# Batched 64-token triangular inverses of an RWKV layer: all four quadrants of the PE array, two tiles half a level apart

## The reference, cut to what matters

```python
def step(state, inp):
    r_t, w_t, k_t, v_t, kk_t, a_t = inp
    sa = jnp.einsum('bhvk,bhk->bhv', state, kk_t)
    state = (state * w_t[:, :, None, :]
             - sa[..., None] * (kk_t * a_t)[:, :, None, :]
             + v_t[..., None] * k_t[:, :, None, :])
    return state, jnp.einsum('bhvk,bhk->bhv', state, r_t)
...
_, y = lax.scan(step, state0, xs)
```

## Time and profile before

| what | us |
|---|---|
| median of 3 runs (2185.68 to 2186.8) | 2185.74 |
| the profiled execution: its time | 2186.04 |
| the profiled execution: span of its instructions | 2184.3 |
| PE busy in the span | 2126.0 |
| first product of round 0, from the span's start | 534.21 |
| first product of round 1 | 569.27 |
| first product of the scan | 605.28 |

### The profile page before, as it was taken

How to read it: one execution, slowest core, us unless ns; L and a number is a source line. 1 busy time by engine, 2 the same in 40 slices (tenths; PEclk the granted TensorE clock), 3 DMA queues, 4 the chain that set the end, 5 groups by cost and what they waited for, 6 DMA issues and landing times. The chain is left out here.

```text
span 2184.3 us, 33539 instructions
## 1 busy us (share of the span) xinstructions
PE 2126.0 (97%) x13592; PEld 1752.4 (80%) x13592; DVE 1134.0 (52%) x1435; ACT 767.3 (35%) x1059; POOL 175.8 (8%) x122
## 2 busy tenths in 40 slices
PE   7999999989989999999999999999999999999998
PEld 6888888768967888888888888877888778888886
DVE  5444444568756544444444444377766665444322
ACT  4222223463333322222322222254554443233221
POOL 2000011001502000001000001101111110000010
PEclk9999999999999999999999999999999999999999
DMA  4222322310012222333222232221111122222321
GB/s 166 96 96 96 122 93 68 108 58 21 5 60 78 96 96 96 103 107 98 77 96 96 96 118 93 78 88 49 40 40 50 50 68 97 96 96 96 116 93 52
DMA packets 48271, 182.75 MB, mean 84 GB/s; under 512 B 6320, under 2 KB 6576, under 8 KB 48048
## 3 DMA queue, kind: packets, MB, share of 16 engines
q1 hardware_dynamic: 48176, 181.39, 25.1%
HBM read 179.27 MB, written 2.10 MB: 83 GB/s over the span
## 5 line engine op out<-in xcount | busy, mean ns | idle before, releaser
L570 PE MATMUL banks<-H,WS 128*128 128x512 f32 x1840 | 733.6, 399 | 13.4 <-DVE H L1763 9.7
L571 PE MATMUL banks<-H,WS 128*128 128x512 f32 x1840 | 719.9, 391 | 0.0
L572 PE MATMUL banks<-H,WS 128*128 128x512 f32 x1840 | 719.8, 391 | 0.0
L1167 ACT ACTIVATE WS<-RAW 128x1024 fp32r<-128x1024 f32 (+1 forms) x310 | 349.1, 1126 | 961.0 <-PE banks L572 956.0
L1683 DVE TENSOR_TENSOR WS<-RAW,WS 128x1024 fp32r<-128x1024 f32 (+1 forms) x310 | 405.3, 1308 | 228.1 <-ACT WS L1167 227.8
L570 PEld LDWEIGHTS banks<-H,WS 128*128 128x128 f32 x1840 | 347.6, 189 | 94.0 <-DVE WS L1683 12.0
L572 PEld LDWEIGHTS banks<-H,WS 128*128 128x128 f32 x1840 | 347.4, 189 | 73.7
L571 PEld LDWEIGHTS banks<-H,WS 128*128 128x128 f32 x1840 | 347.5, 189 | 71.1 <-issue 2.4
L570 PE MATMUL banks<-A,WS 128*128 128x512 f32 x704 | 273.9, 389 | 0.0
L571 PE MATMUL banks<-A,WS 128*128 128x512 f32 x704 | 273.9, 389 | 0.0
L572 PE MATMUL banks<-A,WS 128*128 128x512 f32 x704 | 273.9, 389 | 0.0
(11 more groups left out here) (360 smaller groups left out, 1734.1 us busy)
## 6 DMA issues: line engine op xcount, KB each, us to landing
RAW<-in_w_gate SPq DMA_DIRECT2D x88, 512.0 KB, 3.4
RAW<-in_w_up SPq DMA_DIRECT2D x88, 512.0 KB, 3.4
RAW<-in_w_down SPq DMA_DIRECT2D x64, 704.0 KB, 4.0
RAW<-in_c_in SPq DMA_DIRECT2D x32, 512.0 KB, 3.4
RAW<-in_ab_in SPq DMA_DIRECT2D x22, 512.0 KB, 3.4
RAW<-in_ab_out SPq DMA_DIRECT2D x8, 512.0 KB, 4.0
RAW<-in_c_out SPq DMA_DIRECT2D x8, 512.0 KB, 3.5
X<-in_x SPq DMA_DIRECT2D x4, 512.0 KB, 7.3
```

The source lines that it names most:

```text
L570: pe.matmul(bank[:, :], WS[:, 0, s, cols], upper, start=first and j == 0, stop=False)
L571: pe.matmul(bank[:, :], WS[:, 0, s, cols], lower, start=False, stop=False)
L572: mm = pe.matmul(bank[:, :], WS[:, 1, s, cols], upper, start=False, stop=last and j == len(rows) - 1)
L1167: act.activation(WS[:, 0, c % SPLIT, 0:cols], RAW[:, c % RING, 0:cols], ACT.Copy).then_inc(hi_ready, 1)
```

## The change

- Chunks 4 to 7 of the inverse's matrices are stored on the opposite partition half. A product then sends half of its small products through the off-diagonal quadrants (`four_ways`). Outputs lie in half banks: chunks 0 to 3 in the first and 4 to 7 in the second bank of a pair (`head_block`, `two_banks`).
- XX is turned by three DVE transposes in place of one (`turned_across`).
- The pair masks go from TM (POOL, each level) to U (DVE, on the way out of PSUM: `minus_by_head`). POOL makes TM once for each tile and round (`triangle`); DVE makes XT from it (`first_turn`).
- PE's order: U of tile 0, XX of tile 1 of the level before, one extra product (`beside`), U of tile 1, XX of tile 0, one extra product. The products of `matrices` and `inside` are spread over the levels; round 1's first product stands in level 4 of round 0.
- The turns of KF go ahead of the levels of round 0, those of AL ahead of and into round 1 (not crossed).
- `branch`, `branch_lo` and `fold` go from DVE to POOL. BV goes ahead of the last `z_block`, one factor product (AL) from block 20 to block 19. The first products don't wait for the last `z_block`. The third `bon_mm` product waits for two copies of the turned VF.
- In the scan the operands of chunks 4 to 7 are read from the other half.

Left out below: the small helpers of the half banks, the semaphore table, most removed lines (they stand in the functions above), and the wrappers of three copies.

```diff
@@ -635,46 +643,52 @@
...
+            lo_half, hi_half = slice(0, CHUNK), slice(CHUNK, P)
+            four_ways = [(r, crossed(r) if c >= TT else r, c) for k in range(TT) for c in (k, TT + k) for r in (lo_half, hi_half)]
...
+            def tokens_turned(first, src, b, upper, across):
...
+                for r, a, c in four_ways:
+                    tr = pe.matmul(head_block(first, a if across else r, c, upper), src[r, b, c * CHUNK:(c + 1) * CHUNK],
+                                   con("ident")[r, r], start=True, stop=True)
                 tr.then_inc(tr_mm, 1)
...
+            def pe_level_u(q, z, l):
+
+                w = INV[z]
+                if l == 0:
+                    pe.wait_ge(x1_turned[z], q + 1)
+                    pe.wait_ge(tm_ready[z], q + 1)
+                    if q == 0:
+                        pe.wait_ge(tr_read, (8, 6)[z])
+                    elif z == 0:
+                        pe.wait_ge(xx_read[z], 5)
                     else:
-                        pe.wait_ge(xx_read[z], 5 * q + l)
...
+                        pe.wait_ge(tr_read, 10)
+                    for r, c in chunk_blocks():
+                        mm = pe.matmul(head_block(4 * z, r, c), w["TM"][r, c, :], w["XX"][r, c, :], start=True, stop=True)
+                else:
+                    pe.wait_ge(xx_read[z], 5 * q + l)
+                    for a, f, c in four_ways:
+                        mm = pe.matmul(head_block(4 * z, f, c), w["TM"][a, c, :], w["XX"][a, c, :], start=True, stop=True)
+                mm.then_inc(u_mm[z], 1)
+
+            def pe_level_xx(q, z, l):
+
+                w = INV[z]
+                pe.wait_ge(iu_ready[z], 5 * q + l + 1)
+                if l:
+                    pe.wait_ge(xt_turned[z], 4 * q + l)
+                if l == 4:
+                    for r, c in chunk_blocks():
+                        mm = pe.matmul(head_block(4 * z, r, c, upper=True), w["IU"][r, c, :], w["XT"][r, c, :], start=True, stop=True)
+                elif l:
+                    for a, f, c in four_ways:
+                        mm = pe.matmul(head_block(4 * z, a, c, upper=True), w["XT"][f, c, :], w["IU"][f, c, :], start=True, stop=True)
+                else:
+                    for r, c in chunk_blocks():
+                        mm = pe.matmul(head_block(4 * z, r, c, upper=True), w["XT"][r, c, :], w["IU"][r, c, :], start=True, stop=True)
+                mm.then_inc(xx_mm[z], 1)
 
@@ -748,55 +762,96 @@
...
+                            for first, b in ((6, 0), (2, 2)):
                                 aux_free(20 + b)
-                                tokens_turned(aux_bank(20 + b), VF, b)
+                                aux_free(21 + b)
+                                tokens_turned(first, VF, b, upper=False, across=True)
+                                tokens_turned(first, VF, b + 1, upper=True, across=True)
...
+                                if b == 2:
+                                    pe.wait_ge(tr_read, 2)
...
-                    pe.wait_ge(z_read, AB_BLOCKS)
...
+                    def matrix(q, z, k):
...
+                        left, right = ((AL, CPRE), (KF, CPRE), (KF, RF), (AL, RF))[k]
+                        if k == 2:
+                            pe.wait_ge(token_read[z], 2 * q + 1)
+                        elif k == 3:
+                            pe.wait_ge(token_read[z], 2 * q + 2)
+                        elif q or k:
+                            pe.wait_ge(mat_ready[z], 4 * q + k)
                         elif z:
...
+                        for r, a, c in four_ways:
+                            cc = slice(c * CHUNK, (c + 1) * CHUNK)
+                            if k < 3:
+                                mm = pe.matmul(head_block(4 * z + 2, a, c), left[r, b, cc], right[r, b, cc], start=True, stop=True)
+                            else:
+                                mm = pe.matmul(BANK[4 * z + 2][r, cc], left[r, b, cc], right[r, b, cc], start=True, stop=True)
+                        mm.then_inc(mat_mm[z], 1)
...
+                    def inside(q, z, k):
...
+                        pe.wait_ge(mat_ready[z], 4 * q + 2 + k)
+                        for r, a, c in four_ways:
                             cc = slice(c * CHUNK, (c + 1) * CHUNK)
-                            mm = pe.matmul(BANK[4 * z + 1][r, cc], TKM[z][r, c, :], VT[r, b, cc], start=True, stop=True)
+                            if k == 0:
+                                mm = pe.matmul(head_block(4 * z + 2, r, c), TKM[z][a, c, :], VT[a, b, cc], start=True, stop=True)
+                            else:
+                                mm = pe.matmul(head_block(4 * z + 2, r, c), VT[a, b, cc], MKM[z][a, c, :], start=True, stop=True)
                         mm.then_inc(token_mm[z], 1)
...
+                    def beside(q, l, z):
+
+                        if l == 0:
+                            inside(q, z, 0)
+                        if l == 1:
+                            matrix(q, z, 2)
+                        if l == 2:
+                            inside(q, z, 1)
+                        if l == 3:
+                            matrix(q, z, 3)
+                        if l == 4 and q == 0:
+                            matrix(1, z, 0)
+                        if l == 4 and q:
+                            pe.wait_ge(mat_ready[z], 8)
+                            tokens_turned(4 * z + 2, AL, 2 + z, upper=False, across=False)
...
                     for q in range(2):
...
+                        if q == 0:
+                            matrix(0, 0, 0)
+                            matrix(0, 1, 0)
+                            tokens_turned(4, KF, 2, upper=False, across=True)
+                            tokens_turned(4, KF, 3, upper=True, across=True)
+                        matrix(q, 0, 1)
+                        matrix(q, 1, 1)
+                        if q == 0:
+                            pe.wait_ge(z_read, AB_BLOCKS)
+                            tokens_turned(0, KF, 0, upper=False, across=True)
+                            tokens_turned(0, KF, 1, upper=True, across=True)
+                        else:
+                            pe.wait_ge(xx_read[1], 5)
+                            tokens_turned(4, AL, 0, upper=False, across=False)
+                            tokens_turned(4, AL, 1, upper=True, across=False)
                         for l in range(5):
-                            pe_inverse_level(q, l, 4 * (q + 1), 2 * (q + 1))
+                            pe_level_u(q, 0, l)
+                            if l:
+                                pe_level_xx(q, 1, l - 1)
+                            beside(q, l, 0)
+                            pe_level_u(q, 1, l)
+                            pe_level_xx(q, 0, l)
+                            beside(q, l, 1)
+                        pe_level_xx(q, 1, 4)
@@ -818,6 +873,7 @@
@@ -827,7 +883,8 @@
...
+                                a = crossed(r) if c >= TT else r
+                                mm = pe.matmul(BANK[1][r, b * CHUNK:(b + 1) * CHUNK], KT[a, b, cc], VT[a, b, cc], start=True, stop=True)
@@ -1209,19 +1266,46 @@
...
+            def level_copied(q, z, l):
+
+                act.wait_ge(xx_mm[z], 5 * q + l + 1)
+                act.activation(by_head(INV[z]["XX"]) if l < 4 else row_by_head(XTF[:, 2 * q + z, :]), two_banks(4 * z, upper=True),
+                               ACT.Copy).then_inc(xx_read[z], 1)
...
             def act_inverse(q):
...
+                if q == 0:
+                    for b, written in ((2, 6), (3, 6), (0, 8), (1, 8)):
+                        tokens_copied(KT, b, 2 * b if b % 2 == 0 else 2 * b - 2, b % 2 == 1, written)
+                else:
+                    for b in range(2):
+                        tokens_copied(BT, b, 4, b == 1, 10)
                 for l in range(5):
...
+                    if l:
+                        level_copied(q, 1, l - 1)
+                    if l in (0, 2):
+                        inside_copied(q, 0, l // 2)
+                    if l == 4 and q:
+                        tokens_copied(BT, 2, 2, False, 11)
+                    level_copied(q, 0, l)
+                    if l in (0, 2):
+                        inside_copied(q, 1, l // 2)
+                    if l == 4 and q:
+                        tokens_copied(BT, 3, 6, False, 12)
+                    if q == 0 and l in (1, 3):
                         branch_hi(l - 1)
...
+                        branch_hi(l)
+                level_copied(q, 1, 4)
@@ -1611,26 +1688,31 @@
...
+            def triangle(q, z):
+
+                w = INV[z]
+                pool.wait_ge(mat_ready[z], 4 * q + 1)
+                if q:
+                    pool.wait_ge(u_mm[z], 5 * q)
+                pool.tensor_tensor(w["TM"][:, :, :], w["TT"][:, :, :], half("ident"), ALU.subtract).then_inc(tm_ready[z], 1)
...
+            def branch(b):
+
+                pool.wait_ge(silu_done, b + 1)
```

(99 more changed lines are left out.)

142 lines of the change are left out of this document (15 added, 127 removed).

## The result

| | before | after |
|---|---|---|
| median, us | 2185.71 (2184.36 to 2189.06, 6 runs) | 2178.41 (2175.68 to 2179.53, 6 runs) |
| profiled execution, us | 2186.04 | 2178.15 |
| ratio after/before | | 0.9967, interval 0.9957 to 0.9977 |

The change makes the kernel 7.3 us faster, against a forecast of 14.1. The sign was right; the time lies 1.4 us above the range of 2168 to 2177.

A forecast was written before the change was run, and what follows sets the result against it. It took the inverse, alone between projections and scan, as the bound, with PE's pace setting a level. Savings of -7.0 by round 0's first crossed turn grew to -14.55 by round 1's, -14.1 at the scan: 2171.6 us median, range 2168 to 2177.

The forecast's parts named there:

- The start: VF's turns to round 0's first product: crossed turns -1.65, a copy wait +0.5, no `z_block` wait; 532.2 instead of 534.21.
- the front of round 0: First product to level 1's first turn: 8 products ahead of U, not 12; turn at 543.0, -7.0 with the start.
- Prices: Unit costs: crossed product 0.52 us for 0.93, crossed turn with IU 1.38, XT 1.30 while POOL works, fold 2.2.
- Levels 1 to 4: Inverse levels: DVE cycle 3.96, PE and ACT cycle 4.16, masked level 5.16; 4.0 to 5.2 us against 4.99.
- PE's own work is at most 3.5: Levels 1 to 4: PE's work per level at most 3.5 us, below the cycles of 3.96 and 4.16.
- DVE idle in the levels: Sign that the forecast is wrong: DVE idling in the levels would mean that hops or PE decide.
- So these levels cost what they cost before: Round 1's levels and the end: from -14.55 at its first crossed turn to -14.1 at the scan, at 591.2.
- rival 1: Inverse levels: hand-overs slower than the rows, 0.2 instead of 0.1, two loops catching on each other; 2175 us, chance 0.14.
- Rival 2: Making XT on DVE isn't held up by POOL, 0.69 four times, -2.4 us; 2169 us, chance 0.09.
- Rival 3: Crossing doesn't pay because the quadrants don't run at once; level cycle 5.74 us, time 2184, no change; chance 0.05.
- Rival 4: PE's clock falls to 1.2 GHz within the inverse; level cycle 6.24 us, time 2193, slower; chance 0.04.
- The 25 ns of the Trainium skill: Matmul starts never closer than about 25 ns: crossed product 0.8 us, cycle 5.28, time about 2178; chance 0.02.

The follow-up runs named there:

- e2: Changed kernel with MKM, MBT and the second `inside` product issuing one of 16 small products each, 360 matmuls less, results not computed: 2172.32 us, ratio 0.9936.
- e11: The changed kernel run once more, unchanged: 2177.51 us, ratio 0.9966 (8 runs).
- e1: Changed kernel with each crossed product's small products reordered, so only two quadrants work at a time within one product: 2179.70 us, ratio 0.9971.
- e6: Changed kernel plus 32 crossed products of 64 columns (1024 matmuls), waiting for nothing, just ahead of the scan: 2212.89 us.
- e8: Changed kernel plus 32 uncrossed products of 64 columns (two quadrants), waiting for nothing, just ahead of the scan: 2212.68 us.
- e4: Changed kernel with only the first of the crossed turn's three DVE transposes left, XT of chunks 4 to 7 staying old: 2179.01 us, ratio 0.9965.
- e7: Changed kernel plus 32 crossed products of 128 columns, waiting for nothing, just ahead of the scan: 2207.85 us.
- e5: Changed kernel with TKM and MKM merged into wider matmuls and unread chunk 7 turns left out, 160 matmuls less, all results kept: 2174.25 us, ratio 0.9951.
- e9: Changed kernel with the burst of 32 crossed products of 64 columns ahead of the scan, executed a second time unchanged: 2208.07 us.
- e10: Changed kernel with the burst of 32 crossed products of 128 columns ahead of the scan, executed a second time unchanged: 2210.61 us.
- e3: Changed kernel with MKM, MBT and the second `inside` product issued twice, 384 matmuls more, results kept: 2191.25 us, ratio 1.0025.

## Why the forecast was half right

- **The start** (2.3 shorter, forecast 2.0) and **the front of round 0** (11.06, forecast 10.8): right, by the steps given. The third `bon_mm` product waited 0.86 for ACT's copies.
- **Prices**: crossed product 0.47 to 0.52, crossed turn 0.44 + 0.89 with IU 1.38 behind its start, XT under POOL 1.29, 1.66 and 1.86 (one of four 0.68, begun 0.17 us before POOL's next piece), a fold 1.68 to 2.13 (estimate 2.2): right, and the last fold ended before the scan. That XT was sometimes over 1.30 cost nothing that can be seen: e2 has it too.
- **Levels 1 to 4: the step that failed.** "PE's own work is at most 3.5" priced PE by the array's time. A level issues six products, 192 matmuls, 1.5 blocks; at 3.65 that is 5.5 us, above both loops of the forecast (3.96 on DVE, 4.16 through ACT) and above the masked level (5.16). From level 1 to level 4 that is 4.5 blocks, 16.4 us; the trace has 17.2 in round 0 (541.11 to 558.32) and 16.5 in round 1 (572.83 to 589.33), where the forecast had 14.6. Most of it came in level 3 (7.5 and 6.2 for 5.2), where DVE waits for the MBT products. (These are not crossed, so that even the array needs 4 x 0.52 + 2 x 0.93 = 3.9 in that level, not "at most 3.5".) The forecast's own sign, DVE idle in the levels, is there: 7.6 us of waits between 541 and 596. So PE's instruction stream sets the pace in both rounds' levels wherever extra products stand in them, and in round 1's front. The sum for the whole inverse is 18 x 3.65 = 65.6 where the forecast had 59.0: 6.6 us, nearly the whole miss (66.8 in e11, 18 x 3.71). The 3.65 isn't only this quotient: PE goes on after the first stop at 533.75 and after the last at 588.58, 15 blocks later, 3.66 each. e2 shows it from the other side: 2.8 blocks fewer, 58.8.
- **"So these levels cost what they cost before"** (the end, 20.7): 22.84. The forecast put extra products into round 1's levels as free filling. They were the costly part.
- **Where the 7.3 come from.** 2.3 from the start, of which 0.6 is lost again in e1 (18.33 in place of 17.69), and 5.5 from the inverse. How the 5.5 divide between the quadrants and the order isn't shown: e1 takes back only half of the crossing (and loses 1.3 by the medians), and no run has uncrossed products in the new order. In the bursts crossing gains 1.8 us of 31.1 (e6 against e8), and before the change the inverse took 4.0 us more than its uncrossed products need (71.1 for 18 x 3.73 = 67.1). That speaks for the order, two tiles half a level apart and overlapping rounds, as the larger part. By stretches of the two profiled executions: -1.9 above the change, -2.3, -4.8, -3.3, +2.6 and +1.7 from the scan on, in sum -7.9, their difference in span.
- **Rivals.** Of the four times rival 1's (2175) is the nearest, by another mechanism, which e2 and e4 refute. Rival 2 fails by XT's rows, and e4 shows that DVE's time isn't the bound. Rival 3 named what mattered, that "the dense levels issue crossed products oftener than mixer C", but not why: the quadrants do run at once, their instructions don't come fast enough. Mixer C's rows, from which the price was taken, are two products that fit in one block. Rival 4: PEclk stayed 1.00.
- **The 25 ns of the Trainium skill.** "TensorE: Matmul & The Clock Gate" would have given about 2178, and 2178.4 was measured, but that is luck: its rule that starts never come closer isn't what the runs show. e6 executes 128 matmuls in 2.09 us, 16 ns each. Over whole blocks the supply makes it 27 to 30 ns.
- **The signs in the profile before.** Mixer C's two products started 0.52 apart, but two in a row don't show a rate. In the levels 128 matmuls took 3.73 us and PE was full; what stood right behind that as the next limit could not be read from busy time, nor from the count of instruction packets (14 in 56 us, one in 4.0), which only shows how fast PE used them. But two short stops of this kind stood in that trace, and were not read:

```profile
554.73 0.73 PE L672 MATMUL banks<-IU,XT 64*64 64x64 f32 x17 [0.20 <-issue]
589.70 1.08 PE L672 MATMUL banks<-IU,XT 64*64 64x64 f32 x29 [0.39 <-issue]
```

  They lie within a product and say that at 3.73 us a block the supply already fell short at times.

What stays open: why a packet starts only 1.1 us or more after PE has gone on, why its start and transfer vary (blocks of 3.3 to 3.9 us, often 3.34, 3.61 or 3.88) in executions of one program, and whether weight loads and matmuls count alike; every matmul here has its load.

## What to carry to other kernels

Price a dense stretch of small matmuls twice, by the array and by its instructions: in these runs 128 matmuls with their loads took 3.5 to 3.9 us (27 to 30 ns a pair) over any longer stretch, though the array did them in 2.09. Below that pace, faster quadrants (e6 against e8) or fewer columns (e6 against e7) give about 2 us of 31; fewer, wider matmuls do (e5: 160 fewer, 4.2 us). A price read from two products in a row is no rate: look in the trace for the longest run without a pause, and for stops at equal counts.

## What the runs showed of the hardware that was not expected

- PE stops within a product, every 128 matmuls with loads, when it uses them faster than they come: 1.36 to 1.64 us a block in e6 at the full clock, with only six instruction packets of 16 KB and almost no other DMA traffic between 608 and 629 us.
- The next block is later while data moves. The stop of 3.70 us in e6 (603.4 to 607.1) lies where the output projection's weights arrive, as the windows of that stretch show:

```profile
604.00:605.00 1.00, 0.00 (x0) 0.00 (x0) 0.00 (x0) 0.00 (x0) 0.00 (x0) 1.00 1.03 406
605.00:606.00 1.00, 0.00 (x0) 0.00 (x0) 0.00 (x0) 0.00 (x0) 0.00 (x0) 1.00 0.96 385
```

  At the same place e9 stops 3.70, e7 and e10 1.56 and e8 1.07 us, longer than anywhere else in their bursts. The packet of that block starts 6.02 us after the one before in e6, not 3.45 to 3.75 as the others of the burst, and then takes 0.95 us like them: it is its start that is late. Five executions agree; the transfer was not moved to test it.
- The pace of the supply differs between executions of one program: the same inverse of 18 blocks took 64.5 to 69.8 us. That is more than the 1.8 us that crossing gains in the bursts, so small edits of a stretch bound in this way need many executions.
- Through stops of up to 1.92 us (e3) the granted clock stayed at 1.00. After the stop of 3.70 us it was at 0.50 for some 3 us, in e6 (607 to 609.6) and in e9 (605 to 608), and PE was busy before it came back. It cost nothing there, for the supply was slower still.
